# Three more TensorE products ahead of the last gate products, four in place of one ahead of the last up products

## What is computed

```python
def expert_block(args):
    xt, e = args
    hid = jax.nn.silu(xt @ w_gate[e]) * (xt @ w_up[e])
    return hid @ w_down[e]
...
x = layer_norm(DEEPNORM_ALPHA * x + mix, ln_g[i, 0], ln_b[i, 0])
ffn = grouped_moe(x, router_w, router_b, w_gate[i], w_up[i], w_down[i])
x = layer_norm(DEEPNORM_ALPHA * x + ffn, ln_g[i, 1], ln_b[i, 1])
```

## Time and profile before

| | us |
|---|---|
| median of 3 executions | 1193.33 |
| lowest, highest | 1193.14, 1196.06 |
| the profiled execution | 1195.33 |
| its span (first to last instruction) | 1193.5 |
| TensorE busy (product rows) in the span | 1014.6 |
| last pair, gate to spread, layer 0 | 555.03 to 579.48 |
| last pair, gate to spread, layer 1 | 1158.67 to 1184.56 |

### The profile page before, as it was taken

The page is one execution under the profiler, slowest core; times in us unless marked ns, Lnnn a source line. Parts: engine busy times, 40 slices in busy tenths (PEclk is TensorE's granted clock), DMA queues, the critical chain, the costliest instruction groups (busy, mean ns, idle before and its releaser), DMA issues.

```text
span 1193.5 us, 18920 instructions
## 1 busy us (share of the span) xinstructions
PE 1014.6 (85%) x7872; PEld 565.5 (47%) x7872; DVE 356.2 (30%) x888; ACT 184.5 (15%) x474; POOL 55.7 (5%) x133
## 2 busy tenths in 40 slices
PE   9999999976698966678899999999866898766765
PEld 7595544543343533344599655444533434423432
DVE  4745612221111111111567775213111111111112
ACT  1023211100010100000321663111100000000001
POOL 1012010000000000000100230100000000000000
PEclk9999999987799987789999999999977899878898
DMA  9937899999999999999992719999999999999994
GB/s 352 373 142 288 343 394 419 426 427 429 427 427 427 428 427 428 428 424 423 371 362 84 283 35 364 391 418 427 427 427 426 428 427 427 427 427 427 427 423 191
DMA packets 59351, 449.12 MB, mean 376 GB/s; under 512 B 4579, under 2 KB 10980, under 8 KB 32636
## 3 DMA queue, kind: packets, MB, share of 16 engines
q1 hardware_dynamic: 57248, 442.52, 90.2%
q0 software_dynamic: 1680, 4.88, 1.2%
q10 hardware_dynamic: 332, 0.42, 0.1%
HBM read 446.72 MB, written 1.07 MB: 375 GB/s over the span
## 4 chain that ended last, share of the span: by engine, by line
PE 55%; DMA 40%; DVE 2%; ACT 1%; issue 1%; SPq 1%; DVEq 0%
PE bank L1220 15%; DMA ring<-in_moe_w_up 14%; DMA ring<-in_moe_w_down 11%; DMA ring<-in_moe_w_gate 10%; PE bank L1001 7%; PE bank L1184 5%; PE bank L1072 5%; DMA bias<-in_moe_w_up 5%; PE bank L1305 3%; PE bank L1281 2%; PE bank L1469 2%; PE bank L1320 2%; PE bank L1041 1%; PE bank L1292 1%; PE bank L1496 1%; PE bank L1063 1%
## 5 line engine op out<-in xcount | busy, mean ns | idle before, releaser
L1220 PE MATMUL bank<-ring,work 128*32 128x256 f32 (+1 forms) x2656 | 336.4, 493 | 106.9 <-DMA ring<-in_moe_w_gate 35.5
L1220 PEld LDWEIGHTS bank<-ring,work 128*32 128x32 f32 (+1 forms) x2656 | 154.5, 136 | 244.4 <-issue 217.2
L1950 DVE TENSOR_TENSOR work<-work,bank 128x256 f32<-128x256 f32 (+1 forms) x32 | 15.6, 488 | 520.6 <-PE bank L1220 520.6
L1305 PE MATMUL bank<-ring,work 128*32 128x512 f32 x576 | 91.9, 627 | 11.6 <-DMA ring<-in_moe_w_down 7.2
L1220 PE MATMUL bank<-softmax_area,work 128*32 128x256 f32 (+1 forms) x352 | 65.8, 503 | 33.8 <-DMA ring<-in_moe_w_gate 25.4
L1963 DVE TENSOR_TENSOR xs<-xs,bank 128x512 f32<-128x512 f32 x112 | 71.1, 684 | 41.8 <-PE bank L1323 23.6
L1220 PE MATMUL bank<-bias,work 128*32 128x256 f32 (+1 forms) x384 | 78.1, 499 | 0.0
L1184 PE MATMUL bank<-work,acc 128*128 128x128 f32 (+1 forms) x448 | 75.5, 323 | 0.0
L1184 PEld LDWEIGHTS bank<-work,acc 128*128 128x128 f32 x448 | 66.0, 191 | 16.6 <-issue 11.5
L1220 PEld LDWEIGHTS bank<-softmax_area,work 128*32 128x32 f32 (+1 forms) x352 | 31.9, 141 | 66.6 <-issue 60.9
L2388 ACT COPY work<-bank 128x256 f32<-128x256 f32 (+1 forms) x32 | 13.6, 425 | 319.4 <-PE bank L1257 252.3
(11 more groups left out here) (331 smaller groups left out, 1273.9 us busy)
## 6 DMA issues: line engine op xcount, KB each, us to landing
ring<-in_moe_w_gate SPq DMA_DIRECT2D x44, 2048.0 KB, 29.2
ring<-in_moe_w_up SPq DMA_DIRECT2D x40, 2048.0 KB, 28.6
ring<-in_moe_w_down SPq DMA_DIRECT2D x36, 2048.0 KB, 29.2
softmax_area<-in_moe_w_down SPq DMA_DIRECT2D x8, 2048.0 KB, 25.1
ring<-in_moe_w_down SPq DMA_DIRECT2D x12, 1024.0 KB, 8.4
ring<-in_moe_w_gate SPq DMA_DIRECT2D x12, 1024.0 KB, 9.3
bias<-in_moe_w_gate SPq DMA_DIRECT2D x6, 2048.0 KB, 34.6
softmax_area<-in_moe_w_up SPq DMA_DIRECT2D x6, 2048.0 KB, 27.7
```

The lines of the kernel that those rows point to most:

```text
L1220: last = mm(bank[2 + k][row:row + cap, 0:width], xgT_of(group_of[i])[:, t, at + e * cap:at + (e + 1) * cap], w[e](t)[:, part * width:(part ...
L1305: last = mm(bank[5][row:row + CAP_NARROW, :], hidT_narrow[:, m, CAP_NARROW * e:CAP_NARROW * (e + 1)], w[e](m)[:, n * 512:(n + 1) * 512], s ...
```

## The change

```diff
@@ -1232,6 +1232,8 @@
                     return
                 if "gate" in blocks:
                     pe.wait_ge(silu_ready, PAIRS * l + i)
+                    if i == PAIRS - 1:
+                        keep_warm(3, b=2)
                     block(0, range(KT)).then_inc(gate_done, 1)
                     if i == 2:
                         spread(l, 0)
@@ -1241,7 +1243,7 @@
                 pe.wait_ge(pickwT_ready, PAIRS * l + i)
                 if i == PAIRS - 1:
                     acc_to_psum(l)
-                    keep_warm(1, b=3)
+                    keep_warm(4, b=3)
                 block(1, range(KT)).then_inc(up_done, 1)
```

## The result

| | us | n |
|---|---|---|
| before, median (lowest to highest) | 1193.38 (1191.91 to 1196.06) | 9 |
| changed, median (lowest to highest) | 1197.60 (1196.45 to 1199.79) | 9 |
| ratio changed to before, 95% interval | 1.0041 (1.0033 to 1.0050) | |
| profiled execution, changed (before 1195.33) | 1198.88 | |
| its span (before 1193.5) | 1197.0 | |

The change costs 4.2 us. The forecast was a gain of 1.05 us, and the range ended at 1195.5.

A forecast was written before the change was run, and what follows sets the result against it. Arrival of weights was taken to bound the experts, with only layer 1's tail open to TensorE. Layer 0 at 0 and layer 1 at -1.05 us took the median from 1193.33 to 1192.3 us; range 1190.9 to 1195.5.

The forecast's parts named there:

- I take the present size: Pair 14's up products, both layers: the stops behind the jump were assumed to stay as long as in the trace.
- the rival named in the prediction: Code behind the jump comes later: another 2.0 us of stop in each layer, +1.9 us in all, 1195.2 us; 12%.
- With it, I expect, the low clock: Layer 1, pair 15: with the idle time gone, the up products take 3.66 us and end 1.49 us earlier.
- The gain is 1.05 us: Layer 1, down products: the last quarter's landing at 1179.68 us limits the 1.49 us gain to 1.05 us.
- Nothing to win in most runs: Layer 1's low clock may be an accident of one execution; otherwise the difference is 0, 1193.3 us; 25%.
- the price of the products: Added work on TensorE: 2.68 us for three ahead of the gate, 3.60 us for four ahead of the up products.
- that layer 0's up products would be late and covered only up to 0.6 us: Layer 0: up products start 1.05 us late; the last quarter's 1.67 us wait absorbs it, leaving 0.6; net 0.
- that the last quarter's landing bounds the end: Layer 1, last eight down rows: weights land at 1179.68 us, giving a new wait of about 0.4 us.
- larger "issue" gaps in pair 14: Mark in pair 14 for the 12% rival that the code behind the jump comes later.
- one of the signs that were to prove the step wrong: Layer 0's wait for the last down quarter was to fall from 1.67 to about 0.6 us; zero would disprove the step.

The follow-up runs named there:

- with only 8 products ahead: The change plus 4 products of never-run padding in layer 0, moving the stops to 8 and about 4 of 64: 1200.13 us, ratio 1.0051 to the kernel before.
- the products alone: Against the kernel before, added products only in the arm that runs; the arm jumped over stays as before: 1194.61 us, ratio 1.0011.
- the four products ahead of the up block alone: Four products ahead of the up products, none ahead of the gate products, code behind the jumps where the changed kernel has it: 1193.76 us, ratio 0.9999 to before.
- At the old place: The change plus never-run padding (58 and 52 products), so code behind the jumps has moved 256 and 512 instructions from the kernel before: 1194.72 us, ratio 1.0007.
- the place alone: Against the kernel before, added products only in the arm that is jumped over, so only the code behind the jump moves: 1193.24 us, ratio 0.9997.
- the kernel before at the start of a block: The kernel before plus never-run padding (16 and 12 products) putting code behind the jumps at a 256-instruction block's start: 1192.69 us, again 1192.76; ratios 0.9995, 0.9996.
- the change at the start of a block: The change plus 10 products of never-run padding in layer 0, code behind both jumps at a block's start: 1192.41 us, again 1192.80; ratios 0.9987, 0.9998 to before.
- the two halves of the change: Three products ahead of the gate, or four ahead of the up products, code behind jumps placed as in the changed kernel: 1194.41 and 1193.76 us; ratios 1.0007, 0.9999 to before.

## Why the prediction was wrong

**The step that failed: "I take the present size"** of the stops behind the jump. The prediction had the shift right (24 and 72 instructions) and the rows, and did not join them. 24 instructions are 12 of the product rows, one LDWEIGHTS and one MATMUL each: 28 - 12 = 16, and 47 - 36 = 11, where 12 was measured. A stop that ends when the next block is there, not after a fixed wait, gets longer by all that no longer fits ahead of it. The time from the first product to the end of the stop was 4.4 us in layer 0 before (539.76 - 535.35), 4.7 after, 4.7 with only 8 products ahead; in layer 1 5.2, 4.7 and 5.0. Over all runs with a stop it lies between 3.7 and 5.7. So the earlier trace rows alone could have given the new sizes, as an estimate: what runs ahead of the stop now takes 1.9 us, so 4.41 - 1.93 = 2.5 us in layer 0 and 5.24 - 1.92 = 3.3 in layer 1, 5.8 in all, where 2.73 and 2.79 were measured. The sum of the rival named in the prediction does well with the true sizes. For layer 0 it gives 1.05 + 1.93 - 1.67 = 1.3 us, for layer 1 -1.05 + 4.29 - 0.44 = 2.8; the two traces show 41.39 - 40.38 = 1.0 and 43.48 - 40.88 = 2.6.

The end of the stop is fixed still better from the jump. The jump comes right behind pair 14's gate products, so the idle time in the bracket of the first up product counts from there. Idle time and time to the end of the stop together are 6.19 + 4.41 = 10.60 and 5.28 + 5.24 = 10.52 us before, 11.02 and 11.04 in the changed kernel, and 9.9 to 11.0 in all fifteen stops of the profiles. That also accounts for the missing stop of the products alone: after 7.27 us of idle time, and 3.6 us for the 28 products ahead of the boundary, 10.9 us had passed.

**Second, the products behind the stop.** The prediction's rival added a stop but no clock. After it, layer 1's 52 products take 6.07 us. The windows of those products (columns as in the earlier trace rows):

```profile
541.19:545.16 3.97, 3.97 (x48) 2.15 (x47) 0.00 (x0) 0.00 (x0) 0.00 (x0) 0.67 1.02 429
1140.80:1142.72 1.92, 1.92 (x12) 0.63 (x13) 0.00 (x0) 0.00 (x0) 0.00 (x0) 0.50 1.02 435
1145.52:1151.59 6.07, 6.07 (x54) 3.18 (x53) 0.00 (x0) 0.00 (x0) 0.00 (x0) 0.52 1.00 424
```

Layer 1's are at 1.2 GHz nearly throughout (0.52), where the kernel before had the second part of the block back at 2.4 GHz (17 rows in 1.27 us). Of the 4.29 us more in layer 1 (10.72 us in place of 6.43), the stop itself is 1.83 and the lower clock the rest; in layer 0 the 64 products took 5.97 us both times, and all of the 1.93 is the stop. This part varies from run to run: the products behind a stop of 1.8 to 3.9 us were granted 0.52 to 0.67 on average, and 0.67 behind the 3.65 us with the four products ahead of the up block alone. The price of the rival, 2.0 us in each layer, was therefore 0.07 too high in layer 0 (1.93) and 2.3 too low in layer 1 (4.29), and its chance of 12% too low for a shift that the rows already fixed.

**Third, the gain that was to be lost.** "With it, I expect, the low clock" goes: it did, 3.66 us in both layers. "The gain is 1.05 us": not there. At the old place the change measured 1.0007 (0.9998 to 1.0016). The idle time ahead of the up products of layer 1 was 3.11 us at the low clock in one profile, but the profile of the place alone shows 2.09 us of idle time and 3.66 us for the block: no low clock to win. The two profiles of the kernel before at the start of a block show 3.66 us there too. That is the rival *Nothing to win in most runs*, given 25%, and the change at the start of a block (1192.80, 1192.76 without the products) bears it out. How often that block runs at the low clock in general stays open: one profile of four with this executed work shows it.

**Right:** the price of the products (from start to start 1164.43 - 1161.76 = 2.67 us for three and 568.73 - 565.21 = 3.52 for four, 2.68 and 3.60 forecast); that layer 0's up products would be late and covered only up to 0.6 us; that the last quarter's landing bounds the end once TensorE is early (waits of 0.64 and 0.89 us in the runs above). The mark that was named, larger "issue" gaps in pair 14, is what the trace shows. So is one of the signs that were to prove the step wrong: layer 0's wait for the last quarter, 1.67 us before, is zero.

**What sets the 4.2 us.** Where TensorE waits for the last quarter of the down weights, that quarter's products start 39.5 to 40.4 us behind pair 14's up products in layer 0 and 39.7 to 40.8 in layer 1 (1178.02 - 1137.52 = 40.50, place alone). The changed kernel's TensorE needs 41.39 and 43.48: 1.0 to 1.9 and 2.7 to 3.8 over, of which the kernel before had none in layer 0 and 1.1 us in layer 1 of its profiled execution. Each of the two halves of the change stays within that budget, give or take half a microsecond. So does the whole change without the stop in three of its four profiled layers; in layer 0 of the run at the start of a block, that run's slowest execution, TensorE starts 1.1 us behind the landing. No run has the longer stop in one layer only, so each layer's share of the loss is read from the traces and not tested by itself.

**Open:** what starts the fetch of a block. One 16 KB packet of the instruction queue lies 2.0 to 2.8 us ahead of each of the four restarts: in 537.0 to 537.5 and 1142.5 to 1143.0 of the kernel before, in 538.5 to 539.0 and 1143.0 to 1143.5 of the changed one. In layer 0 of the kernel before it comes ahead of the stop (which begins at 538.96), so the stop is not what asks for it. The DMA engines were busy for about 90% of these windows or more, so whether the fetch is slow or asked for late is not told apart. That the stops are waits for instructions is itself an inference, from their place modulo 256 instructions and from these packets; no row names a releaser.

## What to carry to other kernels

Dead code ahead of a jump's target is not free. Where a trace shows a stop without a releaser behind a jump, note how many instructions run ahead of it. In these runs an edit that moved the target by n instructions moved the stop by as many, with a period of 256, and the fewer ran ahead of the stop, the longer, on the whole, it was. And filling idle time with useless work spends the cover of everything upstream; count the whole path from the first wait, with its stops, against the last landing before filling it.

## What was not expected of the hardware

- A stop without a releaser behind a jump ended 9.9 to 11.0 us after TensorE's last product ahead of the jump, in all fifteen cases, whether 4 or 48 products had run ahead of it.
- A stop in the middle of a block of products can also put off the return of the clock: the changed kernel's first 12 up products of pair 14 in layer 1 ran at 0.50, and behind the stop of 2.79 us the other 52 took 6.07 us at a granted clock of 0.52, while in the kernel before the 36 and 17 rows behind stops of 0.80 and 0.96 us ran at 1.00.
- Padding that never runs moved the median from 1192.4 us (10 products; 1192.8 when run again) over 1197.6 (none) to 1200.1 (4): a range of 0.6% from the place of code alone.
